# Filler projections of a recurrence, in portions of eight K tiles at every second step

## The reference

```
(na_q, ..., rw_r, rw_k, rw_v, rw_gate, rw_lw, rw_la, merge_logits) = split(h @ w_in)
S = S * w_t + (S @ a_t) b_t^T + v_t k_t^T ;  y_t = S @ r_t        # 16 heads of 64, each direction
g_na, g_pool, g_rw = split(sigmoid(merge_logits), 3)
merged = g_na * (b_na @ w_branch[0]) + g_pool * (b_pool @ w_branch[1]) + g_rw * (b_rw @ w_branch[2])
out = merged @ w_out
```

## Time and profile before

| | |
|---|---|
| median of the runs | 4277.61 us |
| the profiled execution | 4284.65 us |
| its span | 4282.9 us |
| TensorE busy | 3720.5 us, 87% |
| VectorE busy | 2097.3 us, 49% |
| ScalarE busy | 1606.3 us, 38% |
| instructions | 84855 |

### The profile page before, as it was taken

The page is one execution under the profiler, slowest core; times in us unless marked ns, Lnnn a source line. Parts: engine busy times, 40 slices in busy tenths (PEclk is TensorE's granted clock), DMA queues, the critical chain, the costliest instruction groups (busy, mean ns, idle before and its releaser), DMA issues.

```text
span 4282.9 us, 84855 instructions
## 1 busy us (share of the span) xinstructions
PE 3720.5 (87%) x36394; PEld 3423.3 (80%) x36394; DVE 2097.3 (49%) x2784; ACT 1606.3 (38%) x2167; POOL 200.8 (5%) x239
## 2 busy tenths in 40 slices
PE   5789659889898799998993888789889999999977
PEld 5678558777787799998993777688689899999977
DVE  4566553343344566665344333325545555556454
ACT  4324223233232455554332333333344444444332
POOL 0030110000000000000000000000110000000000
PEclk8889789999998899999997999899999999999989
DMA  3303005554453345444551322333423333333253
GB/s 126 111 1 129 11 39 209 190 200 175 177 209 113 121 168 172 169 168 158 177 177 63 110 99 95 108 127 111 171 96 114 109 107 103 113 110 105 97 189 127
DMA packets 81706, 551.99 MB, mean 129 GB/s; under 512 B 10448, under 2 KB 10480, under 8 KB 19344
## 3 DMA queue, kind: packets, MB, share of 16 engines
q1 hardware_dynamic: 69984, 497.06, 33.1%
q0 software_dynamic: 11440, 50.66, 3.5%
HBM read 525.66 MB, written 22.02 MB: 128 GB/s over the span
## 4 chain that ended last, share of the span: by engine, by line
PE 48%; DVE 7%; ACT 6%; issue 3%; DMA 1%; ACTq 0%; DVEq 0%; POOL 0%; POOLq 0%; SPq 0%
PE banks L1792 4%; PE banks L270 4%; PE banks L272 4%; PE banks L271 4%; PE banks L1594 3%; ACT w_hi L246 3%; PE banks L1595 2%; PE banks L1596 2%; PE banks L284 2%; PE banks L285 2%; PE banks L286 2%; PE banks L1095 2%; PE banks L1097 2%; PE banks L1096 2%; DVE w_lo L252 2%
## 5 line engine op out<-in xcount | busy, mean ns | idle before, releaser
L252 DVE TENSOR_TENSOR w_lo<-ring,w_hi 128x2048 fp32r<-128x2048 f32 x343 | 785.8, 2291 | 1178.5 <-ACT w_hi L246 1178.5
L270 PE MATMUL banks<-x_hi,w_hi 128*128 128x256 f32 x3344 | 961.8, 288 | 85.0 <-DVE w_lo L252 34.7
L271 PE MATMUL banks<-x_lo,w_hi 128*128 128x256 f32 x3344 | 951.7, 285 | 1.7 <-issue 1.7
L272 PE MATMUL banks<-x_hi,w_lo 128*128 128x256 f32 x3344 | 951.2, 284 | 0.0
L246 ACT CAST w_hi<-ring 128x2048 fp32r<-128x2048 f32 x343 | 653.4, 1905 | 345.1 <-PE banks L1097 184.7
L270 PEld LDWEIGHTS banks<-x_hi,w_hi 128*128 128x128 f32 x3344 | 647.3, 194 | 139.3 <-issue 76.7
L271 PEld LDWEIGHTS banks<-x_lo,w_hi 128*128 128x128 f32 x3344 | 647.6, 194 | 1.9 <-issue 1.9
L272 PEld LDWEIGHTS banks<-x_hi,w_lo 128*128 128x128 f32 x3344 | 647.1, 194 | 0.0
L1650 DVE TENSOR_TENSOR w_lo<-ring,w_hi 128x512 fp32r<-128x512 f32 x316 | 217.3, 689 | 267.7 <-ACT w_hi L1607 266.6
L1594 PE MATMUL banks<-xk_hi,w_hi 128*128 128x256 f32 x1024 | 318.2, 311 | 13.9 <-DVE w_lo L1650 13.8
L1595 PE MATMUL banks<-xk_lo,w_hi 128*128 128x256 f32 x1024 | 291.7, 285 | 0.0
(11 more groups left out here) (479 smaller groups left out, 6674.9 us busy)
## 6 DMA issues: line engine op xcount, KB each, us to landing
ring<-in_w_up SPq DMA_DIRECT2D x88, 1024.0 KB, 4.9
ring<-in_w_dil SPq DMA_DIRECT2D x72, 1024.0 KB, 4.9
mod_ring<-in_w_mod SPq DMA_DIRECT2D x48, 1024.0 KB, 6.8
ring<-in_w_logit SPq DMA_DIRECT2D x48, 1024.0 KB, 4.9
ring<-in_w_down SPq DMA_DIRECT2D x44, 1024.0 KB, 4.9
ring<-in_w_delta SPq DMA_DIRECT2D x32, 1024.0 KB, 4.9
ring<-in_w_out SPq DMA_DIRECT2D x32, 1024.0 KB, 4.8
ring<-in_w_na SPq DMA_DIRECT2D x32, 1024.0 KB, 4.7
```

Source lines behind the costliest of these rows:

```text
L252: nc.vector.tensor_tensor(w_lo[:, s, 0:w], ring[:, s, 0:w], w_hi[:, s, 0:w].bitcast(F32), ALU.subtract).then_inc(S("panel_split"), 1)
L270: nc.tensor.matmul(out_ap, hi, xh, start=k == 0, stop=False)
L271: nc.tensor.matmul(out_ap, hi, xl, start=False, stop=False)
L272: last = nc.tensor.matmul(out_ap, lo, xh, start=False, stop=k == tiles - 1)
```

## The change

`F` is no longer one step of the generator. In each of the three programs a counter goes up at every call; at odd counts nothing happens, at even counts the generator is moved twice. A portion is so eight K tiles, 24 matmuls, two casts and two subtractions, at every second call, and the calls between are empty. The counter runs through all groups, so a given step has its portion in some groups and none in others. The work left at the end is moved as before. Nothing else is changed: the marks of the recurrence, the order of the panels and all waits are the same.

```
+    def in_pairs(fill):
+        turn_ = [0]
+
+        def step_():
+            turn_[0] += 1
+            if turn_[0] % 2 == 0:
+                next(fill, None)
+                next(fill, None)
+        return step_
+
     def rw_pe(pe, fill):
-        F = lambda: next(fill, None)
+        F = in_pairs(fill)
...
     def rw_act(act, fill):
-        F = lambda: next(fill, None)
+        F = in_pairs(fill)
...
     def rw_dve(dve, ch, fill):
-        F = lambda: next(fill, None)
+        F = in_pairs(fill)
```

## The result

The changed kernel took **4334.26 us** (median of 4333.15 and 4335.38) against 4277.61 before: ratio 1.0132, 95% interval 1.0108 to 1.0156, 56.7 us slower. A second set of runs beside the experiments gave 1.0131 (1.0115 to 1.0146). The forecast was 4348 us, with a range of 4312 to 4398.

A forecast was written before the change was run, and what follows sets the result against it. TensorE was taken as the bound. Terms -43.1 + 92.9 + 8 - 5 + 1.4 + 16 = +70 us, so 4355 us profiled, 4348 us as median, 1.6% slower; range 4312 to 4398.

The forecast's parts named there:

- TensorE is the bound and its filler is the cover: Recurrence stage: TensorE busy 939.4 of 968.0 us, with filler matmuls covering the evictions; 28.6 us idle.
- Which steps lose their cover: 96: Of 154 emptied steps in the groups, 96 have a handover that waits for a tile just evicted.
- Their price, +92.9 us: Uncovered handovers of the recurrence at 0.95, 1.02, 0.85 or 1.14 us each: +92.9 us on 96 steps.
- lateness, +8: Paired casts and subtractions in ScalarE's and VectorE's queues make some results late: +8 us, between 0 and 25.
- Joining, -43.1 us: Joining two filler portions on TensorE saves 0.28 us at each of 154 emptied steps: -43.1 us.
- Old waits relieved, -5 us: Late splits, 13.8 us of waiting on line 1594, gain slack since a split now has two steps: -5 us.
- the shifted first portion, +1.4: The last of five portions ahead of the first group moves behind it, where TensorE already waited 1.42 us: +1.4 us.
- The clock, +16 us: One in five of 56 filler-free stretches drops TensorE's clock: 11 falls of 1.5 us, +16 us; bounds 0 and 84.
- Not slower: Rival, chance 0.05: empty steps turn out covered, mean uncovered wait under 0.45 us; 4235 us, at best 4206.
- The clock swings: Rival, chance 0.22: over 20 of the 56 filler-free stretches end at half clock; 4362 to 4416 us.
- The queues: Rival, chance 0.10: doubled casts behind table loads delay evictions in most groups, 34 us in place of 8; 4374 us.
- Its signs of being wrong: Stage: TensorE idle grows under 50 us, clock under 0.96, or line 1650 ends more idle than the recurrence's evictions.

The follow-up runs named there:

- the same joins at harmless and at needed places: Against the kernel before: 42 aligned joins where the next step needs nothing just made, -5.8 us; 36 aligned joins after ya, +30.8 us.
- portions of sixteen: Sixteen K tiles at every fourth step, in place of the changed kernel's eight at every second: +136.9 us over the kernel before, ratio 1.0323.
- the first version of the harmless joins: Kernel before with 56 joins only, at steps whose next step needs nothing just made, some portions straddling two panels: +4.4 us, ratio 1.0008.
- the kernel on odd counts: The changed kernel with its doubled portions on odd counts in place of even ones: +47.8 us over the kernel before, ratio 1.0109.

## Why the prediction was right, and by how much each step missed

- *TensorE is the bound and its filler is the cover.* Right. The pair "TensorE joined alone, +50" and "splits joined alone, +19" shows it, and so does the pair of the same joins at harmless and at needed places, -6 and +31.
- *Which steps lose their cover: 96.* Nearly right, and the equal number is luck: 93 of the 96 showed, three did not, and three others took their place, two of them an old wait that moved.
- *Their price, +92.9 us, and lateness, +8.* The 93 take 102.8 us, 98.2 above the regular 93 x 0.05, for 100.9 forecast with both terms. The single ones read 0.96, 1.05, 0.85 and 1.15 us in the timeline for 0.95, 1.02, 0.85 and 1.14. Nine of them were late, 0.3 to 1.5 us over the shortest of their kind and some 7 us in all. The forecast put that down to the paired casts; with single casts some 3 us remain, so the size is right and the reason only in part. The gap behind the last y adds 1.
- *Joining, -43.1 us.* Entries and exits of filler fell by 69.7 us. Of these, 14 are old waits that are gone (next point). Added back: 5 us of regular distance at the 96 gaps, 10 at the harmless empty steps (they cost 0.15 to 0.2, not 0.05), and a change of about -1 within filler. That leaves some -42. Right.
- *Old waits relieved, -5 us, and the shifted first portion, +1.4.* **Mis-sized**: 19 waits of over 0.6 us around filler, 23.0 us in all, became two of 5.8, which is -14 net of the regular distances. Of that, 6 us is the wait for KDs, which only moved to between products. That leaves -8 for -3.6. The wait of the first step grew by 2.9 us (the earlier trace rows has 1.42) and not by 1.4:

```profile
PE banks L1821 <- DVE small L2133: 4.3, 1, 4.3
```

  The empty step gives each split two steps of slack. The price of the opposite, splits without slack, is in the +19 of the kernel with the splits joined alone.
- *The clock, +16 us.* **Mis-sized**: six falls more than before, with 7.2 us more in filler at the lower level. I had allowed 11 falls of 1.5 us, one in five of the regular stretches. None of those led to a fall; the nearest old row, three quarters busy and no fall, was the right guide for them. The falls came with the late handovers, which the forecast of the clock left out. The rule of the Trainium skill ("TensorE: Matmul & The Clock Gate", section "A second HAM failure mode: psum-queue depth-cycling"), told there of another kernel, says that frequent short idle times between groups make the gate swing. Here 96 gaps of about 1 us and more in 1020.9 us left the clock at 0.98, and the measurement decides.
- *Sum.* 98 + 1 - 42 - 8 + 7 = +56 for the 56.0 of the table. The forecast's +70 was too high by 9 us of clock, 4 of old waits and 2 of lateness and price.
- *Rivals.* Not slower: wrong, since mean uncovered time is 1.1 us, not under 0.45. The clock swings: wrong here, and only in part right for portions of sixteen. The queues: at most a few us in the changed kernel. The result lies in the forecast's own bracket, 4325 to 4362.
- *Its signs of being wrong.* None showed: TensorE's idle time in the stage grew by 70 us, the clock is 0.98, and line 1650 ended 7.7 us of idle time.
- *What the forecast did not see* is that alignment of portion and panel matters at all. It did not change this result, since the counter keeps them aligned, but it cost the first version of the harmless joins some 10 us.

What stays open is a part of why the kernel on odd counts is 7 us faster than the changed one. Some 4 us of it are the first step: with portions on odd counts six stand ahead of it in place of four, and TensorE waits there 0.23 us from filler to product, not 4.58. The two waits for KDs between products are 4.7 us in all for 6.0. The rest was not tried.

## What to carry to other kernels

Independent work between a product and the next one that waits for its eviction is worth the eviction's length up to once, and nothing beyond: spread it in portions a little longer than the eviction over just those steps, and join portions only where the next product needs nothing new. When portions grow or move, check where a portion crosses from one prepared buffer to the next, as its preparation needs a step of slack. Count the handovers from the waits in the code and price them from one timeline; here 93 of 96 counted ones showed. Look for the late ones too: in the changed kernel the clock fell behind those alone.

## What the runs showed of the hardware

A product of 64x64 blocks takes 0.05 us from its last start to the next product's first, but 0.15 to 0.2 us where the next one has another shape or is filler, and 0.21 from filler back; a filler portion pays 0.11 us once more at its second matmul. Joining 56 portions saves 21.0 us at entries and exits and gives 10.8 back at the transitions of the products. The granted clock held at 0.98 with TensorE idle for a tenth of the time, mostly in pieces of 1 us, and fell to 0.94 with filler-free stretches of 8 us. Each fall from 2.4 to 1.2 GHz cost 1.1 us in filler matmuls.
